# Sample rows by quadrants, and two blocks instead of six, in a fused decoder layer

## What is computed

```
shift1, scale1, gate1, shift2, scale2, gate2 = split(c @ w_ada + b_ada, 6)   # per request: 1 prompt row, 8 sample rows
h = rms_norm(x, g_pre_mix) * (1 + scale1) + shift1
z = h @ w_in                                  # mLSTM q,k,v,o,i,f; attention q,k,v; two merge gates
hm, C, n, m = mlstm_branch(z...)              # chunked recurrence over 64 tokens
hd = diff_branch(z...)                        # softmax(q1 k1) v - lam * softmax(q2 k2) v, RMS norm per head
merged = sigmoid(gm) * (hm @ w_proj_m) + sigmoid(gd) * (hd @ w_proj_d)
y = merged @ w_out
x = x + gate1 * rms_norm(y, g_post_mix)
h2 = rms_norm(x, g_pre_ffn) * (1 + scale2) + shift2
a, b = split(h2 @ w_up, 2)                    # D_FF = 2816 each, D_MODEL = 1024
f = (gelu(causal_conv3(a) + conv_b) * b) @ w_down
x = x + gate2 * rms_norm(f, g_post_ffn)       # outputs y_prompt, y_sample, and the new caches and states
```

## Time and profile before

| | us |
|---|---|
| median of 3 runs | 1788.15 |
| lowest and highest | 1787.59, 1788.34 |
| the profiled execution | 1788.27 |
| its span in the trace | 1786.5 |
| PE busy in it | 1742.0 (98%) |
| DVE, ACT, POOL busy | 751.9 (42%), 501.3 (28%), 155.2 (9%) |

### The profile page before, as it was taken

The page is one execution under the profiler, slowest core; times in us unless marked ns, Lnnn a source line. Parts: engine busy times, 40 slices in busy tenths (PEclk is TensorE's granted clock), DMA queues, the critical chain, the costliest instruction groups (busy, mean ns, idle before and its releaser), DMA issues. The chain is left out here.

```text
span 1786.5 us, 27232 instructions
## 1 busy us (share of the span) xinstructions
PE 1742.0 (98%) x11459; PEld 1649.1 (92%) x11459; DVE 751.9 (42%) x1018; ACT 501.3 (28%) x811; POOL 155.2 (9%) x231
## 2 busy tenths in 40 slices
PE   6999999999999999999999999999999999999998
PEld 5899988888888899989978899999999999999997
DVE  6422144544530246455544344424434434334345
ACT  5311144434343334431233321121211211211212
POOL 4100000000010015300023200000000000000001
PEclk9999999999999999999999999999999999999999
DMA  9665332241247586352632111111111111021004
GB/s 340 220 205 182 131 112 93 92 130 64 88 122 229 154 258 150 91 140 103 216 107 74 65 48 48 50 45 48 48 48 48 35 60 48 24 65 53 24 30 170
DMA packets 159721, 190.26 MB, mean 106 GB/s; under 512 B 13697, under 2 KB 138129, under 8 KB 159608
## 3 DMA queue, kind: packets, MB, share of 16 engines
q1 hardware_dynamic: 139432, 171.17, 30.0%
q10 hardware_dynamic: 19168, 17.21, 3.0%
q0 software_dynamic: 1008, 0.23, 0.1%
HBM read 146.70 MB, written 41.87 MB: 106 GB/s over the span
## 5 line engine op out<-in xcount | busy, mean ns | idle before, releaser
L158 PE MATMUL ps<-mg_hi,w_hi 128*128 128x352 f32 x1008 | 218.1, 324 | 2.0 <-ACT a_ext L2755 2.0
L158 PE MATMUL ps<-mg_hi,w_lo 128*128 128x352 f32 x1008 | 217.3, 323 | 0.0
L158 PE MATMUL ps<-mg_lo,w_hi 128*128 128x352 f32 x1008 | 217.0, 323 | 0.0
L158 PEld LDWEIGHTS ps<-mg_hi,w_hi 128*128 128x128 f32 x1008 | 171.6, 189 | 2.5 <-issue 1.9
L158 PEld LDWEIGHTS ps<-mg_hi,w_lo 128*128 128x128 f32 x1008 | 173.1, 188 | 0.0
L158 PEld LDWEIGHTS ps<-mg_lo,w_hi 128*128 128x128 f32 x1008 | 171.2, 188 | 0.0
L2848 DVE TENSOR_TENSOR f_t<-f_t,ps 128x1056 f32<-128x1056 f32 x80 | 100.2, 1253 | 151.3 <-PE ps L158 151.3
L143 DVE TENSOR_TENSOR w_lo<-w_raw,w_hi 128x2048 fp32r<-128x2048 f32 x60 | 139.0, 2316 | 50.8 <-ACT w_hi L139 50.8
L139 ACT ACTIVATE w_hi<-w_raw 128x2048 fp32r<-128x2048 f32 x60 | 114.8, 1914 | 121.0 <-PE ps L158 120.0
L1258 PE MATMUL ps<-acts_hi,w_hi 128*128 128x352 f32 x384 | 132.8, 346 | 6.0 <-ACT out_z L1108 3.8
L1374 PE MATMUL ps<-acts_hi,w_hi 128*128 128x352 f32 x384 | 128.0, 333 | 4.6 <-PEq L1027 1.6
(11 more groups left out here) (415 smaller groups left out, 3059.9 us busy)
## 6 DMA issues: line engine op xcount, KB each, us to landing
w_raw<-in_w_in SPq DMA_DIRECT2D x22, 1024.0 KB, 5.5
w_raw<-in_w_up SPq DMA_DIRECT2D x22, 1024.0 KB, 5.1
w_ada_chunks<-in_w_ada ACTq DMA_DIRECT2D x16, 1024.0 KB, 8.4
w_raw<-in_w_down SPq DMA_DIRECT2D x11, 1024.0 KB, 4.8
z_scratch<-out_z SPq DMA_DIRECT2D x48, 176.0 KB, 1.8
z_scratch<-gate_ev SPq DMA_DIRECT2D x48, 176.0 KB, 3.7
w_ada_chunks<-in_w_ada SPq DMA_DIRECT2D x8, 1024.0 KB, 11.6
chunks<-z_scratch SPq DMA_DIRECT2D x24, 256.0 KB, 4.2
```

The costliest lines, as they stand in the source:

```text
L158: mm = pe.matmul(ps[:, bank + b, 0:TB], w[wi][:, k, j * P:(j + 1) * P], (a_hi, a_lo)[ai][:, k, b * TB:(b + 1) * TB], start=(n == 0), stop= ...
```

## The change

There are three parts.

1. *Conditioning columns by quadrant.* Each quadrant j now makes its own 128 of a pair's 512 columns and sums over all eight k tiles, so a pair is 32 fp32 matmuls of 128 columns instead of 16 of 256, nothing is left to add across quadrants, `ada_row` is 128x128 and one matmul against `sel4` (132 columns) takes the place of four. Each chunk is now half of the k tiles of both parts of the pair, loaded by one DMA or by two of half the size.
2. *The samples' tile by quadrant.* The samples' 32 rows by 1024 columns stand as 128 partitions by 256, quadrant q holding columns 256 q and on. Their products are fp32 matmuls with the raw weights (`sample_tile`, 32 matmuls of 256 columns, with `mg_s`; `last_down` with `g_s`, 8 matmuls), sums over a token's four quadrants come from a matmul with `same_tok` (`quad_sums`, `F_SUM`), and loads and stores of these rows are four DMAs each, or one on the scratch `X1S`. Samples are now the first tile (`SAMPLES = 0`) in mix and in the tail.
3. *Two blocks.* First part and attention are one block, decode, recurrence, mix and feed-forward the other. At each of the four inner joints every engine ends its part with a drain that raises a semaphore (`first_ended` and so on, in the order SP, ACT, DVE, PE, POOL), and the engines wait for chosen ones of these. At the joint after the first part PE waits for DVE only, and only before `scores(0)`; the other engines wait for all. After decode PE waits for DVE, the others for all. After the recurrence only ACT waits, for DVE. After mix SP and POOL wait for ACT and DVE.

The core of the diff:

```diff
+    def all_ended(engine, ended, own):
+        for n, x in enumerate(ended):
+            if n != own:
+                engine.wait_ge(x, 1)
...
         def load_ada(eng, n):
-            eng.dma_start(w_ada[:, n % WS, :].rearrange("p (k n) -> p k n", k=KT), ada_cols(n)).then_inc(s_wada[n % WS], 16)
+            halves = ada_rows(n)
+            for s, src in enumerate(halves):
+                dst = ada_slot(n)[:, :, s:s + 1, :] if len(halves) == 2 else ada_slot(n)
+                eng.dma_start(dst, src).then_inc(s_wada[n % WS], 16)
...
-                act.activation(ada_row[:, p % 2, :], ps[:, BA, :], ACT.Copy).then_inc(s_arow, 1)
+                act.activation(ada_row[:, p % 2, :], ps[:, BA, 0:P], ACT.Copy).then_inc(s_arow, 1)
...
-                        for kk in range(2):
+                    for k in range(KT // 2):
                             for j in range(4):
-                                mm = pe.matmul(ps[32 * j:32 * j + 32, BA, n % 2 * NC_:(n % 2 + 1) * NC_], c_t[:, 2 * j + kk, :],
-                                               w[:, 2 * j + kk, :], start=(kk == 0), stop=(kk == 1), skip_group_check=True)
+                            mm = pe.matmul(ps[32 * j:32 * j + 32, BA, 0:P], c_t[:, n % 2 * (KT // 2) + k, :],
+                                           w[:, k, j // 2, j % 2 * P:(j % 2 + 1) * P], start=(n % 2 == 0 and k == 0),
+                                           stop=(n % 2 == 1 and k == KT // 2 - 1), skip_group_check=True)
...
-                    for i in range(4):
-                        tr = pe.matmul(ps[:, BT, i * TOK_C:(i + 1) * TOK_C], ada_row[:, p % 2, i * P:(i + 1) * P], sel[:],
+                tr = pe.matmul(ps[:, BT, 0:4 * TOK_C], ada_row[:, p % 2, :], sel4[:].rearrange("p j t -> p (j t)"),
                                        start=True, stop=True)
...
                 z_half(1)
+                pe.wait_ge(first_ended[2], 1)
                 scores(0)
...
+            sp.wait_ge(tile_done, TILE5 + HALF_OF[SAMPLES, 1])
                 for half in range(2):
                     load_chunk(sp, half, up_chunk(0, half), KT, FFN0 - 1 + half)
...
+            dve.wait_ge(merged_lo, KT)
+            dve.tensor_tensor(mg_s[:], mg_hi[:, :, SEQ:T].bitcast(F32), mg_lo[:, :, SEQ:T].bitcast(F32), ALU.add).then_inc(merged_s, 1)
...
+            def sample_tile():
+                w = [x.rearrange("p (k n) -> p k n", k=KT) for x in (w_raw[:, 0, :], w_raw[:, 1, :], xw_raw[0][:], xw_raw[1][:])]
+                for k in range(KT):
+                    for q in range(QUADS):
+                        mm = pe.matmul(ps[TS * q:TS * q + TS, BH + 1, 0:NC_], mg_s[:, k, :], w[q][:, k, :],
+                                       start=(k == 0), stop=(k == KT - 1), skip_group_check=True)
+                mm.then_inc(tile_done, 1)
+            def quad_sums(i):
+                pe.wait_ge((yr_ss, h_ss)[i], SAMPLES + 1)
+                pe.matmul(sum_at(i), same_tok[:], stat(SAMPLES, 3 * i), start=True, stop=True).then_inc(quad_sum, 1)
...
+            sample_tile()
                 pe.wait_ge(w_lo_ready, OUT0 + 4)
                 pe.wait_ge(gated[1], KT)
-                for t in range(2):
-                    half_tile(t, 1)
+            half_tile(1, 1)
+            quad_sums(1)
+            half_tile(2, 1)
...
                     def last_down(t):
+                        if t == SAMPLES:
+                            for k in range(2):
+                                for q in range(QUADS):
+                                    mm = pe.matmul(ps[TS * q:TS * q + TS, 2 * (t % 4), 0:NC_], g_s[:, k, :],
+                                                   w_raw[:, 0, k * D_MODEL + q * NC_:k * D_MODEL + (q + 1) * NC_],
+                                                   start=False, stop=(k == 1), skip_group_check=True)
+                            mm.then_inc(tile_done, 1)
+                            return
...
```

More of the change, by code:

```diff
@@ L89, in build @@
     ident = sb("ident", [P, P])
+    same_tok = sb("same_tok", [P, P])
     mask_q = sb("mask_q", [P, P])
@@ L1211, in _ @@
             def _(pe):
+                first_pe(pe)
                 def fill(f, blocks):
@@ L1769, in _ @@
-                for b in B8:
-                    for pg in range(NPG):
-                        for h in range(H):
-                            mm = pe.matmul(ps[quad(h), 4, 0:P], at[:, pg, h, TS * b:TS * (b + 1)], v_pg[:, b, pg, h * P:(h + 1) * P],
-                                           start=False, stop=(b == DEC_B - 1 and pg == NPG - 1), skip_group_check=True)
-                pes.done(mm, "pv")
-                until(AT_O)
-                dvs.wait(pe, "o_nrm")
-                pes.done(pe.transpose(ps[:, 5, 0:P], o_r[:], ident[:]), "o_cols")
@@ new lines, in scores @@
+                pes.done(mm, ("sc", b))
+            for b in B8:
+                until(AT_K[b])
+                if b:
+                    scores(b - 1)
+                if b == 1:
+                    dvs.wait(pe, "num1")
+                k_transposes(b)
+            until(AT_K[DEC_B])
+            scores(DEC_B - 1)
+            until(AT_PT)
+            dvs.wait(pe, "diff")
+            for pg in range(NPG):
+                pe.transpose(ps[:, 0, pg * P:(pg + 1) * P], e_s[:, 0, pg * P:(pg + 1) * P], ident[:])
@@ new lines, in decode_pe @@
+            for h in range(H):
+                tr = pe.matmul(ps[quad(h), 1, 0:TS], e_s[quad(h), 0, NEWC:NK], ident[quad(h), quad(h)], start=True, stop=True,
+                               skip_group_check=True)
+            pes.done(tr, "pt")
+            until(AT_PV)
+            acs.wait(pe, "ptn")
+            dvs.wait(pe, "at")
+            pe.wait_ge(d_vl, 16 * NPG * DEC_B)
+            for h in range(H):
+                pe.matmul(ps[quad(h), 4, 0:P], atn[quad(h), :], vs_tok[quad(h), :], start=True, stop=False, skip_group_check=True)
@@ new lines, in decode_pe @@
+            for b in B8:
+                for pg in range(NPG):
+                    for h in range(H):
+                        mm = pe.matmul(ps[quad(h), 4, 0:P], at[:, pg, h, TS * b:TS * (b + 1)], v_pg[:, b, pg, h * P:(h + 1) * P],
+                                       start=False, stop=(b == DEC_B - 1 and pg == NPG - 1), skip_group_check=True)
+            pes.done(mm, "pv")
+            until(AT_O)
+            dvs.wait(pe, "o_nrm")
+            pes.done(pe.transpose(ps[:, 5, 0:P], o_r[:], ident[:]), "o_cols")
```

2969 lines of the change are left out of this document (1520 added, 1449 removed).

## The result

The changed kernel takes 1767.82 us (median of 4 runs, 1766.51 to 1769.69) against 1788.15 of the kernel before on the same chip: a ratio of 0.9889, with a 95% interval of 0.9872 to 0.9906. That is 20.3 us less; the forecast was 1766.8, so 1.0 us off. On two further chips its median is 1766.04 and 1765.99, each time 21.2 or 21.3 us under the kernel before.

A forecast was written before the change was run, and what follows sets the result against it. PE was taken to bound the kernel, busy 1742.0 of 1786.5 us. Conditioning 7.4, sample tile of mix 7.0, tail 2.1 and joints 5.0 sum to 21.5 us off 1788.27, giving 1766.8; range 1763.0 to 1771.5.

The forecast's parts named there:

- Conditioning, −7.4: Twelve pairs of chunks: −7.1 from fewer `condition_tr`, ±0 from narrower instructions, −0.3 at the start; bounds −9 and +11.
- ±0 for the 64 instructions: Conditioning pair: 64 instructions of 128 columns take 1.82 us, against 1.87 for 32 of 256, so no change.
- The start's −0.3: First conditioning pairs: the slow-clock stretch can move either way by about 1.8 us; −0.3 was taken.
- Sample tile of mix, −7.0: Samples' tile in mix: 11.1 us of matmuls and 0.7 of transposes go, cheaper quadrant work comes; bounds −6.1 and −7.8.
- Tail, −2.1: Samples' tile in the tail: 4.56 us becomes 1.8, less 0.7 for a larger last store; bounds −2.9 and −1.2.
- Joints, −5.0: Four opened joints lose their barriers: −1.5, −0.8, −0.9 and −1.8 us in order; bounds −3.1 and −6.5.
- a granted clock below 0.9 after 36 us: Sign that the prediction is wrong: PE's granted clock under 0.9 anywhere later than 36 us.
- a wait over 1 us at a joint: Sign that the prediction is wrong: a wait longer than 1 us at one of the joints.
- Joints whose waits only move (1): Joints: waits only move or a drain costs what the barrier did; 1 us instead of 5, 1770.8; chance 0.14.
- More at the start and the joints (2): Slow-clock stretch falls on waits, −1.8, and joints reach their far end, −1.5: 1763.5; chance 0.12.
- Narrow instructions that don't halve (3): Conditioning: each instruction takes its own time whatever its columns, giving back 18.4: 1785; chance 0.05, of which 0.02 slower.
- A part hidden by loads (4): First 50 us: loads set the end of everything, another 2.3 of the conditioning is lost: 1769; chance 0.13.

The follow-up runs named there:

- e1_cond: The kernel before with only the conditioning columns by quadrant and the split loads: 1781.18 us against 1787.25, ratio 0.997.
- after: The changed kernel's first measurement, all three parts against the kernel before: median 1767.82 us against 1788.15; its profiled execution took 1769.09.
- e10_tiles: The kernel before with only the samples' tiles of mix and tail by quadrant, samples first: 1778.06 us against 1787.32, ratio 0.995.
- after_third: The changed kernel repeated unedited on another chip, against the kernel before: 1765.99 us against 1787.32, ratio 0.9881.
- e2_six: The changed kernel with its old joints back, six closed blocks with barriers: 1770.13 us against 1787.25 of the kernel before, ratio 0.9905.
- e5_actfree: The changed kernel with ACT, before mix, waiting only for DVE's last recurrence column: 1767.15 us against 1788.03 of the kernel before, ratio 0.9882.
- e9_beforefill: The kernel before with 18 idle transposes added in PE's pauses at attention's end: 1787.36 us against 1787.32, ratio 1.0002.

## Why the prediction was right, step by step

- **Conditioning, −7.4.** The term of `condition_tr` is right: 0.14 to 0.32 us a pair where 0.23 was taken. So is ±0 for the 64 instructions: 1.88 us where 1.82 was read from the long run of the earlier trace rows. The row with the same number of instructions in a run was the right neighbour, and the row of 8 at a time the wrong one. Behind the pair of the earlier trace rows, part 1 gives 7.05. The start's −0.3 was too small: the pair itself came 1.5 and 1.4 us earlier in the two executions above, and 0.4 later in e1_cond, where x came late. It follows the loads of x, and over all profiles it stands anywhere from 28.08 to 30.00, which is more than the term. By its medians part 1 alone gave 6.1, 1.3 less than this term, on top of part 2 it gave 7.9.
- **Sample tile of mix, −7.0.** Measured −8.1, beyond the bound of −7.8. Each piece was a little high: the tile 3.59 where 3.74 and 0.2 for entry and exit were taken, the two sums 0.28 instead of 0.45, the wait charged for the second sum absent (0.2). What was left out is a wait on hs that the old last tile had; in the waits of PE of the kernel before

```profile
PE ps L2557 <- ACT hs L2389: 1.4, 2, 0.9
```

  became 0.8 in one, 0.6 less. The samples as the last tile had their chain in the open, as the first they don't.
- **Tail, −2.1.** Measured −2.2 in "after" and −1.8 in e10_tiles, with 1.73 us for the tile (1.8 predicted). The last addition ends at 1764.32 and the span 3.1 us later, where it was 2.4: the larger store costs 0.6 where 0.7 was taken (1.1 in e10_tiles).
- **Joints, −5.0.** Part 3 measures 4.1 to 4.7. The first gave 1.56 where 1.5 was taken: the last matmul of the first block and the first of attention start 1.98 us apart before and 0.42 after, which leaves 0.1 of idle time, and DVE's last copy, which would have been late, is covered by PE's `z_half` (DVE still copies when PE goes on):

```profile
206.86 0.32 PE L967 MATMUL ps<-acts_hi,w_lo 128*128 128x352 f32 x1
207.21 0.52 DVE L738 COPY stage_last<-ps 128x352 f32<-128x352 f32 x1 [3.29 <-PE ps L967]
...
207.28 0.42 PE L1297 MATMUL ps<-acts_hi,w_hi 128*128 128x352 f32 x1
```

  The second gave 0.92 where 0.8 was taken: 125.19 became 124.27 in after_third. PE starts 0.31 us after DVE's end, and by the profile what it waits for last is not DVE but ACT's `gate_ev` (635.90 and 0.46 on ACT, so 636.36):

```profile
631.92 4.23 DVE L1707 SCALAR_TENSOR_TENSOR big<-big,dec_bc,ps 128x128 f32<-128x128 f32 x16 [4.19 <-PE ps L1844]
...
635.90 0.46 ACT L1573 ACTIVATE gate_ev<-ps 128x352 f32<-128x352 f32 x1 [4.62 <-PE ps L1414]
...
636.46 0.40 PE L1414 MATMUL ps<-acts_hi,w_hi 128*128 128x352 f32 x1 [0.60 <-ACT gate_ev L1573]
```

  The third, where the prediction gave half back, gave 0.3 to 0.9: barrier and acts_lo waits were 1.93 + 0.39 + 0.67 before, 1.95 + 0.38 in e10_tiles, 1.95 + 0.41 + 0.31 in e2_six, and are 0.26 + 1.80 now. Right in kind, but the reason given was only half of it: ACT's wait for all of DVE holds acts_lo first, and the loads come next (e5_actfree). The fourth gave 1.62 − 0.26 = 1.36 and the second a_ext wait of 0.34, 1.7 where 1.8 was taken; POOL's memsets end at 998.76 and its copy follows at once, beside PE's new work. Joint by joint the rows add up to 4.5 to 5.1, the medians say 4.1.
- **What was not foreseen** is the fall of the clock between attention and decode, 2.7 us in the profiled execution. The prediction looked for a slow stretch only at the start, and the trace of the kernel before had none at this place. The prediction named "a granted clock below 0.9 after 36 us" and "a wait over 1 us at a joint" as signs that it was wrong. Both came, and it was not: the clock fell twice in this execution, and the 1.79 us on acts_lo stand in place of 3.0 of barrier and acts_lo together. Both signs were too strict. A wait at a joint has to be held against all waits that it replaces.
- **The sum.** That it is off by only 1.0 us is in part luck, since several errors cancel: the tile of mix gave 1.1 more than taken, the start about 1 more, the joints up to 0.9 less, and in the profiled execution the clock cost 2.7 ahead of decode and 1.7 to 2.1 in mix. Without falls at these two places the traces are 23.4 us apart (1786.5 and 1763.1), which also pairs a high run of the one with the lowest of the other; the medians say 20.3 to 21.3, where 21.5 was predicted.
- **The rivals.** Joints whose waits only move (1): in part, at the third joint alone, at most 1.6 of its 1.9. More at the start and the joints (2): the start, by about 1. Narrow instructions that don't halve (3): no. A part hidden by loads (4): not seen in the rows, where the pair at 42 us gives its full share, but part 1 alone gave 1.3 less than its term by the medians, so a part of it isn't excluded.

## What to carry to other kernels

On an engine that is 98% busy, a joint with a barrier costs 1.5 to 1.95 us, and without it 0.1 to 0.3 us of idle time remain and the last real input; let the engine that makes that input wait for the one step that it reads, not for the end of another engine's part. Price a narrow instruction from the row with the most of its kind in a run, and put a tile whose chain is long and whose matmuls are few ahead of the others. When a stage of an otherwise equal program gets longer by more than its waits, look at the granted clock of that stretch and at a second execution before looking for a cause in the change.

## What the hardware showed

- fp32 matmuls on quadrants of 32 columns start 29.4 ns apart at 128 columns and 56 to 58 at 256, in runs of 64 and 32. That leaves no room for a fixed cost on top of the columns. With all 128 columns of weights it is otherwise: two instructions took 0.14 us from start to start at 1 column (the sum in mix) and at 132 (`condition_tr`).
- The granted clock fell to the 1.2 GHz level at waits of 0.64, 0.60 and 1.58 us among pieces of work in some executions and not in others of the same kernel. It stayed low for 6.8 us at a cost of 2.5 to 2.7, or for 3.4 at a cost of 1.3 to 1.5. At the start a fall cost about 1.1 (188.10 and 188.01 against 186.96 us up to attention), and in e9_beforefill, where it took the place of waits, nothing.
- A load of the same bytes landed 1.2 to 1.7 us sooner, counted from the stage's start, in variants whose only edits on PE lie more than 120 us ahead; its issue did not move, and the same edit in the kernel before moved nothing. The cause is open.
